# PEER stage: a two-rate schedule for gathered rows, one product operation for three gate parts, and two output tiles finished inside the loop over dense blocks

## The reference, cut to what matters

```python
def peer(h, p, l):
    ...
    s = jnp.einsum('thpd,phkd->thpk', q, p['peer_keys'][l])
    sv, si = lax.top_k(s, PEER_TOPK)
    cand = sv[:, :, 0, :, None] + sv[:, :, 1, None, :]
    ...
    top_s, pos = lax.top_k(cand.reshape(T, PEER_HEADS, PEER_TOPK * PEER_TOPK), PEER_TOPK)
    ...
    gate = jax.nn.softmax(top_s.astype(jnp.float32), axis=-1).astype(h.dtype)
    ...
        act = jax.nn.gelu(jnp.einsum('cd,ced->ce', xc, u_tab[ic]), approximate=False) * gc
        return jnp.einsum('ce,ced->cd', act, v_tab[ic])

x = x + gate2 * peer(h, p, l)
y_prompt = rmsnorm(xp, final_norm); y_sample = rmsnorm(xs, final_norm)
```

## Time and profile before

| | us |
|---|---|
| median of 3 runs (lowest, highest) | 2825.49 (2819.63, 2825.88) |
| profiled execution, whole time | 2825.95 |
| its span (first to last instruction) | 2824.2 |
| granted TensorE clock over the span | 0.907 |

### The profile page before, as it was taken

How to read it: one execution, slowest core, us unless ns; L and a number is a source line. 1 busy time by engine, 2 the same in 40 slices (tenths; PEclk the granted TensorE clock), 3 DMA queues, 4 the chain that set the end, 5 groups by cost and what they waited for, 6 DMA issues and landing times.

```text
span 2824.2 us, 42662 instructions
## 1 busy us (share of the span) xinstructions
PE 2382.7 (84%) x17458; PEld 1613.9 (57%) x17458; DVE 1883.3 (67%) x3842; ACT 426.0 (15%) x831; POOL 913.5 (32%) x774
## 2 busy tenths in 40 slices
PE   5989968678787888897798159999999999998984
PEld 2545527567676774333344157777776677765552
DVE  1111264346688786664679997887899878876776
ACT  2111212133222221001211011000001000000001
POOL 0000000000132231333434201666654656665661
PEclk8999979889899898898899558999999999999997
DMA  8241130130255462656765403999998999999995
GB/s 286 90 179 60 60 112 2 39 112 2 78 167 166 125 202 82 252 194 237 285 223 180 163 1 137 370 374 384 409 364 329 406 394 370 381 377 409 409 409 224
DMA packets 195293, 638.57 MB, mean 226 GB/s; under 512 B 25158, under 2 KB 27078, under 8 KB 194138
## 3 DMA queue, kind: packets, MB, share of 16 engines
q0 software_dynamic: 110592, 402.70, 38.6%
q1 hardware_dynamic: 84506, 233.13, 22.3%
HBM read 627.11 MB, written 8.65 MB: 225 GB/s over the span
## 4 chain that ended last, share of the span: by engine, by line
PE 57%; DVE 19%; DMA 13%; issue 5%; POOL 2%; ACT 2%; SPq 1%; another core or an unknown queue 0%; DVEq 0%; POOLq 0%; ACTq 0%
PE ps L1031 10%; PE ps L1040 10%; DMA arena<-in_peer_v,arena 10%; PE ps L570 6%; PE ps L1051 6%; PE ps L800 3%; PE ps L914 2%; PE ps L947 2%; DVE arena L1809 2%; DVE arena L1805 2%; PE ps L572 2%; POOL arena L2129 1%; DVE arena L1652 1%; DVE arena L1986 1%; DMA arena<-in_w_in 1%
## 5 line engine op out<-in xcount | busy, mean ns | idle before, releaser
L1031 PE MATMUL ps<-arena 128*128 128x256 f32 x2048 | 481.5, 389 | 37.1 <-DMA arena<-in_uT 36.4
L1040 PE MATMUL ps<-arena 128*128 128x512 f32 x1024 | 468.6, 601 | 33.1 <-DVE arena L2027 31.2
L1031 PEld LDWEIGHTS ps<-arena 128*128 128x128 f32 x2048 | 393.1, 195 | 107.1 <-issue 57.3
L2129 POOL DMA_INDIRECT arena<-in_peer_u,arena x256 | 333.5, 1303 | 346.8 <-DVE arena L1773 160.2
L1986 DVE SCALAR_TENSOR_TENSOR arena<-arena 128x1024 f32<-128x1024 f32 x252 | 315.8, 1282 | 74.3 <-DMA arena<-in_peer_v,arena 72.8
L2129 POOL DMA_INDIRECT arena<-in_peer_v,arena x256 | 299.6, 1170 | 201.3 <-DVE arena L1986 145.6
L2117 POOL DMA_INDIRECT arena<-in_peer_u,arena x128 | 128.5, 1004 | 705.7 <-DVE arena L1805 351.2
L1040 PEld LDWEIGHTS ps<-arena 128*128 128x128 f32 x1024 | 194.5, 192 | 237.2 <-issue 230.2
L1981 DVE SCALAR_TENSOR_TENSOR arena<-arena 128x1024 bf16<-128x1024 f32 x256 | 303.5, 1221 | 38.3 <-DMA arena<-in_peer_u,arena 36.1
L1051 PEld LDWEIGHTS ps<-arena 128*128 128x128 bf16 x3072 | 206.9, 157 | 52.8 <-issue 46.9
L800 PE MATMUL ps<-arena 64*64 64x128 f32 x1920 | 191.1, 288 | 40.2 <-DVE arena L1845 32.7
(11 more groups left out here) (351 smaller groups left out, 3270.0 us busy)
## 6 DMA issues: line engine op xcount, KB each, us to landing
arena<-in_uT SPq DMA_DIRECT2D x128, 512.0 KB
arena<-in_peer_v SPq DMA_DIRECT2D x128, 512.0 KB
arena<-in_w_ada SPq DMA_DIRECT2D x12, 2048.0 KB, 11.7
arena<-in_peer_wq SPq DMA_DIRECT2D x8, 2048.0 KB, 9.4
arena<-in_w_in SPq DMA_DIRECT2D x6, 2048.0 KB, 8.1
arena<-in_w_out SPq DMA_DIRECT2D x4, 2048.0 KB, 8.2
arena<-in_peer_u,arena POOLq DMA_INDIRECT x384
arena<-in_peer_v,arena POOLq DMA_INDIRECT x384
```

Of the source, the lines that this page charges most:

```text
L1031: m = pe.matmul(ps[:, 4 + i % 2, 0:ND], us[i % UB][:, k, :], hTd[:, k, :], start=(k == 0), stop=(k == KD - 1))
L1040: m = pe.matmul(ps[:, 2 * r + c, :], sgel[:, i % SBUFS, P * r:P * r + P], vs[i % VB][:, 512 * c:512 * c + 512], start=(i == 0), stop=(i == ...
L2129: pool.indirect_dma_start(gring[:, n % RING, :], None, a[("peer_u", "peer_v")[e]][0], bass.IndirectOffsetOnAxis(ap=ids[:, t, m:m + 1], axi ...
```

## The change

- `rows_by(i)`: before, the 512 rows were spread evenly over blocks 5 to 125 (4.27 a block). Now 400 rows go over blocks 8 to 95 (4.60 a block) and 112 over blocks 95 to 126 (3.61 a block).
- `ROUTE_STEPS`: tile 1's routing is spread over blocks 0 to 8 instead of 0 to 5, tile 2's over 40 to 56 instead of 40 to 52.
- `one_hots`: the three products are one operation on 768 elements, whose first input is read three times; the equality they start from has a buffer of its own, `same_i`, for which DVE waits until its own last product is done.
- `FIN_AT`: tiles 0 and 1 are finished at blocks 104 and 108 (sum in that block, mean in the next, scaling in the one after; on ACT the square in that block, the root in the next). SP loads residual and norm weights at i = 100. Tiles 2, 3 and 4 follow the loop, 3 and 4 interleaved.

```diff
+EARLY = 400
 def rows_by(i):
-    return max(0, min(ROWS, (i - 5) * ROWS // (ETILES - 8)))
+    return max(0, min(EARLY, (i - 8) * EARLY // 87)) + max(0, min(ROWS - EARLY, (i - 95) * (ROWS - EARLY) // 31))
...
-ROUTE_STEPS = {1: (0, 5), 2: (40, 52)}
-FIN_ORDER = (0, 1, 3, 4, 2)
+ROUTE_STEPS = {1: (0, 8), 2: (40, 56)}
+FIN_AT = {104: 0, 108: 1}
...
+        same_i = half(hr(QI * GRP // 2), 1, QI, GRP)
...
-            sp.wait_ge(S("x_out"), 16)
-            sp.wait_ge(S("xc_out"), 16)
-            sp.wait_ge(S("a_ok"), ETILES)
-            sp.dma_start(xr, spill).then_inc(S("ld_xr"), 16)
-            sp.dma_start(fnorm, a["final_norm"].partition_broadcast(P)).then_inc(S("ld_xr"), 16)
...
+                if i == 100:
+                    sp.wait_ge(S("x_out"), 16)
+                    sp.wait_ge(S("xc_out"), 16)
+                    sp.wait_ge(S("a_ok"), (NPART - 1) * QI)
+                    sp.dma_start(xr, spill).then_inc(S("ld_xr"), 16)
+                    sp.dma_start(fnorm, a["final_norm"].partition_broadcast(P)).then_inc(S("ld_xr"), 16)
...
+            def fin_square(t):
+                act.wait_ge(S("x2_ok"), 2 * NLT + t + 1)
+                A(yo[t], xr[:, t, :], ACT.Square, accum_out=stat[:, t:t + 1]).then_inc(S("n2_sq"), 1)
+            def fin_root(t):
+                act.wait_ge(S("sq_mean"), 8 + t + 1)
+                A(stat[:, 16 + t:17 + t], stat[:, 8 + t:9 + t], ACT.Sqrt).then_inc(S("root_ok"), 1)
...
+                if i in FIN_AT:
+                    fin_square(FIN_AT[i])
+                if i - 1 in FIN_AT:
+                    fin_root(FIN_AT[i - 1])
+            fin_square(2)
+            fin_root(2)
+            fin_square(3)
+            fin_square(4)
+            fin_root(3)
+            fin_root(4)
...
-                oi = one_i[g % 2]
-                rown.do(V.tensor_tensor(oi[:, 2, :, :], iota8[:, 0, QI * q:QI * q + QI, :], col(0, QI), ALU.is_equal))
                 V.tensor_tensor(one_j[:, g % 2, :, :], iota8[:, 0, :, :], col(1, P), ALU.is_equal)
+                if g >= 1:
+                    dve.wait_ge(S("one_ok"), g)
+                rown.do(V.tensor_tensor(same_i[:, 0, :, :], iota8[:, 0, QI * q:QI * q + QI, :], col(0, QI), ALU.is_equal))
                 rown.settle()
-                for k in range(2):
-                    m = V.tensor_tensor(oi[:, k, :, :], oi[:, 2, :, :], col(2 + k, QI), ALU.mult)
-                rown.do(m)
-                rown.settle()
-                V.tensor_tensor(oi[:, 2, :, :], oi[:, 2, :, :], col(4, QI), ALU.mult).then_inc(S("one_ok"), 1)
+                V.tensor_tensor(one_i[g % 2], same_i.to_broadcast([P, 3, QI, GRP]),
+                                slot5[:, 2:5, d, c:c + GRP].unsqueeze(2).to_broadcast([P, 3, QI, GRP]), ALU.mult).then_inc(S("one_ok"), 1)
...
+                if t == 2:
+                    dve.wait_ge(S("a_ok"), ETILES)
...
+                if i in FIN_AT:
+                    fin_sum(FIN_AT[i])
+                if i - 1 in FIN_AT:
+                    fin_mean(FIN_AT[i - 1])
+                if i - 2 in FIN_AT:
+                    fin_norm(FIN_AT[i - 2])
...
-                        for _ in range(66 // (hi - lo)):
+                        for _ in range(64 // (hi - lo)):
...
-            for k in range(2):
-                finish(k)
-            for k in range(2, NT):
-                finish(k)
+            fin_sum(2)
+            fin_mean(2)
+            fin_norm(2)
+            fin_sum(3)
+            fin_sum(4)
+            fin_mean(3)
+            fin_mean(4)
+            fin_norm(3)
+            fin_norm(4)
```

More of the change, by code:

```diff
@@ L307, in program @@
         fnorm = at(gmat.offset + NT * D, D)
-        yo = at(gmat.offset + (NT + 1) * D, NT, D)
-        sqj = at(gmat.offset + (2 * NT + 1) * D, NT, D)
+        yo = [at(gmat.offset + (NT + 1 + t if t < 2 else QI * ND // D + t - 2) * D, D) for t in range(NT)]
         ring_at = SB - WBUF * KD * 512
@@ L493, in _ @@
                     load_v(i - 2 + VB)
-            sp.wait_ge(S("x_out"), 16)
-            sp.wait_ge(S("xc_out"), 16)
-            sp.wait_ge(S("a_ok"), ETILES)
-            sp.dma_start(xr, spill).then_inc(S("ld_xr"), 16)
-            sp.dma_start(fnorm, a["final_norm"].partition_broadcast(P)).then_inc(S("ld_xr"), 16)
-            for n, t in enumerate(FIN_ORDER):
-                sp.wait_ge(S("y_ok"), n + 1)
+                if i == 100:
[4 more added lines that the diff above has]
+                    sp.dma_start(fnorm, a["final_norm"].partition_broadcast(P)).then_inc(S("ld_xr"), 16)
+            for t in range(NT):
+                sp.wait_ge(S("y_ok"), t + 1)
                 dst = y_prompt[0] if t == 0 else y_sample[0, P * (t - 1):P * t, :]
-                sp.dma_start(dst, yo[:, t, :]).then_inc(S("out_state"), 16)
+                sp.dma_start(dst, yo[t]).then_inc(S("out_state"), 16)
             sp.wait_ge(S("out_state"), 16 * (16 + NT))
@@ L1379, in _ @@
                         A(dots, dots, ACT.Gelu).then_inc(S("gelu_ok"), 1)
-            for n, t in enumerate(FIN_ORDER):
-                act.wait_ge(S("x2_ok"), 2 * NLT + n + 1)
-                A(sqj[:, t, :], xr[:, t, :], ACT.Square, accum_out=stat[:, t:t + 1]).then_inc(S("n2_sq"), 1)
-                act.wait_ge(S("sq_mean"), 8 + n + 1)
-                A(stat[:, 16 + t:17 + t], stat[:, 8 + t:9 + t], ACT.Sqrt).then_inc(S("root_ok"), 1)
+                if i in FIN_AT:
[8 more added lines that the diff above has]
+            fin_root(4)
         @block.vector
@@ L2027, in weigh, with fin_sum @@
                 V.tensor_tensor(sgel[:, i % SBUFS, :], sgel[:, i % SBUFS, :], gmat[:, i % (2 * QI), :], ALU.mult).then_inc(S("a_ok"), 1)
-            def finish(k):
-                t = FIN_ORDER[k]
-                if k == 0:
+            def fin_sum(t):
+                if t == 0:
                     dve.wait_ge(S("ld_xr"), 32)
+                if t == 2:
+                    dve.wait_ge(S("a_ok"), ETILES)
                 if t >= GT:
@@ L2038, in finish, with fin_mean, fin_norm @@
                     of = h2[:, t, :]
-                rown.do(V.tensor_tensor(yo[:, t, :], of, g2bc[:, min(t, 1), :], ALU.mult))
+                rown.do(V.tensor_tensor(yo[t], of, g2bc[:, min(t, 1), :], ALU.mult))
                 rown.settle()
-                V.tensor_tensor(xr[:, t, :], xr[:, t, :], yo[:, t, :], ALU.add).then_inc(S("x2_ok"), 1)
-                dve.wait_ge(S("n2_sq"), NT + k + 1)
+                V.tensor_tensor(xr[:, t, :], xr[:, t, :], yo[t], ALU.add).then_inc(S("x2_ok"), 1)
+            def fin_mean(t):
+                dve.wait_ge(S("n2_sq"), NT + t + 1)
                 V.tensor_scalar(stat[:, 8 + t:9 + t], stat[:, t:t + 1], 1.0 / D, EPS, ALU.mult, ALU.add).then_inc(S("sq_mean"), 1)
-                dve.wait_ge(S("root_ok"), 8 + k + 1)
+            def fin_norm(t):
+                dve.wait_ge(S("root_ok"), 8 + t + 1)
                 rown.do(V.reciprocal(stat[:, 24 + t:25 + t], stat[:, 16 + t:17 + t]))
                 rown.settle()
-                V.scalar_tensor_tensor(yo[:, t, :], xr[:, t, :], stat[:, 24 + t:25 + t], fnorm, ALU.mult, ALU.mult).then_inc(S("y_ok"), 1)
+                V.scalar_tensor_tensor(yo[t], xr[:, t, :], stat[:, 24 + t:25 + t], fnorm, ALU.mult, ALU.mult).then_inc(S("y_ok"), 1)
             def route_tile(t):
```

## The result

The changed kernel took **2786.67 us** (median; 2784.27 to 2792.53) where the kernel before took 2825.68 beside it: a ratio of 0.9874 [0.9849, 0.9899] over the runs taken together, so 1.26% or some 36 us faster (the two medians lie 39 us apart). A second measurement beside other runs of the kernel before gave 0.9883 [0.9868, 0.9898]. The forecast was 2795 with a range of 2776 to 2819, so the time lies inside it, on the fast side. The profiled execution took 2792.53 us (span 2790.7), which is the slowest of its four; the sum of the prediction answers to that one, and misses it by 2.5 us.

The account below looks back on a forecast made before the run. PE was taken to bound the gate stage and DMA the stage without groups. Last row at 2772 plus an end of 20.8 gave a 2793 us span; with 1.75 around it 2795 us, range 2776 to 2819.

Parts of the forecast that it names:

- What bounds the kernel: Before the change: PE sets the gate stage's pace, DMA at 404 GB/s the last stage's; then a 44.2 us end.
- Part 1: One-hot operations on DVE: 1.37 instead of 1.59 us a group, gaining 2.5 us before the loop, hidden in it.
- rival D: One-hots: the broadcast product runs at half rate; total about 2803, inside the forecast's spread, sharing its chance of 0.58.
- Part 2: Start of the rows: tile 1's indices at about 1772 us, first row taken at about 1785, eight rows landed by then.
- Part 3: Gate stage: 298.8 MB at 404 GB/s take 739.6 us; with 8 us of loss block 96 starts at 2547.
- Rival A: Gate stage: DMA's idle time stays, from DVE's fixed order; block 96 at 2569, total 2817; chance 0.20.
- Rival B: Gate stage: no loss at all, the routing stall gone too; block 96 at 2531, total 2779; chance 0.12.
- C: Gate stage: late block loads stop PE, then DVE and rows; block 96 65 us late, total 2852; chance 0.10.
- Part 4: Stage without gate groups: 91.0 MB at 404 GB/s take 225 us, DMA sets the pace; last row done at 2772.
- Part 5: The end, from last row to end of span: 20.8 us instead of 44.2, a gain of 23.4.

Follow-up runs that it names:

- early_368: The changed kernel with 368 instead of 400 rows in blocks 8 to 95 and 144 after; 2810.25 us, ratio 1.0012 to before.
- early_432: The changed kernel with 432 instead of 400 rows in blocks 8 to 95 and 80 after; 2799.09 us, ratio 0.9971 to before.
- start5_416: The changed kernel with rows from block 5, 416 of them by block 95, tile 1's routing over blocks 0 to 5; 2762.57 us, ratio 0.9840 to before.
- u_finish: The changed kernel with all five tiles finished after the loop and the residual loaded there, as before; 2800.71 us, ratio 0.9933 to before.
- rows_alone: The kernel before with only the new row schedule and routing steps; 2809.67 us, ratio 0.9969 to before.
- u_product: The changed kernel with the three separate one-hot products of before; 2796.36 us, ratio 0.9921 to before; measured again 2780.41 us, ratio 0.9896.
- twice_new: The changed kernel with the three-part one-hot product done twice in each group; 2793.24 us, ratio 0.9961 to before.

## Why the prediction was right, step by step

**What bounds the kernel** held. PE sets the pace of the gate stage and DMA that of the last one, which early_368 and early_432 show from both sides. The price of a block of 6.96 us gave 209 for the last stage of 30 blocks; early_432 took 205.9 and start5_416 208.1.

**Part 1.** The product was forecast at 0.55 us and took 0.56, so rival D is out by measurement. Most groups take 1.40 us where 1.37 was forecast, but most took 1.54 before and not the 1.59 of the one group that the prediction read, so the saving of 0.2 was 0.14. Before the loop 2.5 us were forecast and 2.4 were seen.

**Part 2** was off by 6 to 9 us. The indices came at 1771.15, as forecast (1772). The first row came at 1791.3, not 1782 to 1785; 1.6 us of that is the later start of the loop. The prediction had named the right wait, ACT's exponential behind the gelu of block 10. DVE's and ACT's timelines:

```profile
1790.38 0.29 DVE L1803 TENSOR_REDUCE arena<-arena 128x8 f32<-128x128 f32 x1 [6.60 <-ACT arena L1357]
...
1791.27 1.22 DVE L2000 SCALAR_TENSOR_TENSOR arena<-arena 128x1024 bf16<-128x1024 f32 x1
```

```profile
1788.34 0.39 ACT L1351 ACTIVATE arena<-ps 128x256 f32<-128x256 f32 x1 [4.12 <-PE ps L1055]
1788.74 1.28 ACT L1357 ACT_TABLE_LOAD   x1
1790.04 0.31 ACT L1357 ACTIVATE arena<-arena 128x128 f32<-128x128 f32 x1
```

Between that gelu (1783.84) and the exponential stands the eviction of a gate group (L1351), which waits for PE until 1788.3. The prediction had counted the gelus in ACT's queue and not that.

**Part 3.** 298.8 MB were forecast and 300.4 came, at 395 GB/s against 393. Block 96 was forecast at 2547 and started at 2544.8. Of that, 1.6 us belong to the later start of the one-hots, so 2543.2 is the like figure: 4 us of loss and not 8. Over all executions without a doubled product the 400 early rows cost 6 us in the gate stage (mean 837.8 of six, against 832.1 of three with even rows); 3 to 4 of them are idle time of PE (10.8 against 7.3), the rest is PE's own time, which varies with the clock. The routing of tile 2 again made a stall of the same size (2140 to 2180: PE busy 34.8 of 40, DMA 319 GB/s). Rival A is out: block 96 would have been at 2569. Of the two arguments against it, that much of DMA's idle time was lower demand holds: by an estimate from its bytes at the 409 GB/s of part 4, DMA idles for some 56 us of the stretch before and 25 after. The other, that DVE would wait for rows in place of PE, holds only in part, 14 us of the 45. Rival B had no loss and no stall in the routing, block 96 at 2531. The total can't tell it from the forecast, since 2786.67 lies midway between 2779 and 2795, but the stages can: the stall stayed and block 96 came at 2544.8. C is out for this cut, with its single wait of 1.5 us unchanged. At 432 rows the gate stage does cost 36 us more, but not by the late block loads that C named.

**Part 4** was right for partly wrong reasons. The stage took 225.5 us and 225 were forecast. DMA moved 92.2 MB, not 91.0, and at 409 GB/s, not 404. The two errors cancel, which is luck. The prediction took 404 GB/s for what DMA can do, and misread it: the window of the earlier trace rows ends with 6 us in which the loads run out. The same window in two pieces:

```profile
2541.50:2774.00 232.50, 209.51 (x701) 132.04 (x700) 166.84 (x158) 11.42 (x30) 139.16 (x121) 0.99 1.03 409
2774.00:2780.00 6.00, 5.42 (x18) 2.92 (x16) 4.99 (x4) 0.38 (x1) 0.00 (x0) 1.00 0.47 188
```

The residual's load was priced at 7.8 us, and u_finish shows 8. The two table loads beside a root cost nothing here:

```profile
2617.65 0.38 ACT L1343 ACTIVATE arena<-ps 128x256 f32<-128x256 f32 x1 [5.18 <-PE ps L1035]
2618.05 1.28 ACT L1367 ACT_TABLE_LOAD   x1
2619.35 0.20 ACT L1367 ACTIVATE arena<-arena 128x1 f32<-128x1 f32 x1
2619.57 1.28 ACT L1343 ACT_TABLE_LOAD   x1
2624.54 0.38 ACT L1343 ACTIVATE arena<-ps 128x256 f32<-128x256 f32 x1 [3.69 <-PE ps L1035]
```

After both loads ACT still waits 3.7 us for PE. The root starts 1.30 us after the start of its table load; the 2.66 us a switch of the Trainium skill, "ScalarE: Activation LUTs", section "What ACT_TABLE_LOAD costs", were not paid here.

**Part 5.** 20.8 us were forecast from the last row to the end, and 20.5 came. DVE's timeline of it:

```profile
2770.28 1.23 DVE L2009 TENSOR_TENSOR arena<-arena 128x1024 f32<-128x1024 f32 x1
2771.53 0.42 DVE L2044 TENSOR_TENSOR arena<-arena 128x256 f32<-128x256 f32 x1
2771.99 1.22 DVE L2057 TENSOR_TENSOR arena<-arena 128x1024 f32<-128x1024 f32 x1
...
2778.61 1.22 DVE L2057 TENSOR_TENSOR arena<-ps,arena 128x1024 f32<-128x1024 f32 x1
...
2786.38 1.28 DVE L2071 SCALAR_TENSOR_TENSOR arena<-arena 128x1024 f32<-128x1024 f32 x1
```

The wait of 10.3 us at the first sum is gone, and tile 2 takes 6.6 us (2771.99 to 2778.61), as before.

**The sum of the parts.** Undone one at a time, the rows are worth 16 to 19 us, the finishing 14 to 17 and the product 4: 34 to 40 against 33 to 36 of the whole, so they add up. Put in alone, the rows gave only 9. Each difference is uncertain by 4 us and more across measurements, and of the 11 us that the profiled execution of rows_alone lost in its gate stage about 5 went with the clock; why its median too gained so little was not settled, nor whether the parts help each other. Three forecasts of experiments were missed: rows_alone (9 us, not 13 to 21), u_product as first measured, and twice_new.

**The rule on HBM** of the Trainium skill ("DMA: Bandwidth & Descriptors", section "Where 436 GB/s comes from"), about 358 GB/s for HBM to SBUF, did not bind this one core: 409 GB/s stood for 225.5 us.

## What to carry to other kernels

Cut the span into the stages that have different limits, and move work of the engine that is full in one stage to where it has slack, up to the point at which the price turns: here the 32 rows from 368 to 400 gained 33 us net by the stages, and the next 32 lost 21 with the longer end. The start of the movable work can count as much as its amount: starting the rows three blocks earlier made room for 16 more. Small parts must be compared side by side; two ratios to a common baseline from two measurements told 11 to 13 us for an edit worth 4. And a rate to be used as a limit must come from a stretch without an empty edge: 404 GB/s was the mean of 409 and of 6 us that had little left to load.
